# Diffusion step on one core: adaLN gates, scale and shift rows by broadcasting DMAs from DRAM instead of one-hot matmuls

## What is computed

```
sh_a, sc_a, g_a, sh_f, sc_f, g_f = _ada(c, w_ada[i], b_ada[i])
h = _modulate(x, sh_a, sc_a)                       # layernorm(x) * (1 + scale) + shift
...                                                # attention or Fourier mix, giving out
x = _post_norm(x, g_a * out, ln_gain[i, 0], ln_bias[i, 0])   # layernorm(ALPHA * x + g * out) * gain + bias
h = _modulate(x, sh_f, sc_f)
moe = _hier_moe(h, w_rg, w_re, w_g, w_u, w_d)
x = _post_norm(x, g_f * moe, ln_gain[i, 1], ln_bias[i, 1])
```

## Time and profile before

| | |
|---|---|
| median of 3 runs | 1095.87 us |
| profiled execution: its time, its span | 1099.61 us, 1097.9 us |
| PE busy | 862.1 us (79%) |
| PE weight loads busy | 463.3 us (42%) |
| VectorE, ScalarE, GpSimd busy | 349.5, 164.2, 140.1 us |
| DMA | 310.20 MB, mean 283 GB/s |
| mean granted TensorE clock | 0.912 |
| chain that ended last, by engine | PE 49%, DMA 33%, DVE 9%, SP's queue 4%, issue 4% |

### The profile page before, as it was taken

The page is one execution under the profiler, slowest core; times in us unless marked ns, Lnnn a source line. Parts: engine busy times, 40 slices in busy tenths (PEclk is TensorE's granted clock), DMA queues, the critical chain, the costliest instruction groups (busy, mean ns, idle before and its releaser), DMA issues.

```text
span 1097.9 us, 14316 instructions
## 1 busy us (share of the span) xinstructions
PE 862.1 (79%) x5177; PEld 463.3 (42%) x5178; DVE 349.5 (32%) x859; ACT 164.2 (15%) x339; POOL 140.1 (13%) x212
## 2 busy tenths in 40 slices
PE   3699999987996787988777864999679887877850
PEld 2465665655555332333323323675543333323320
DVE  2103656566365211111111117445521101111118
ACT  0112221122101111110111113210211111011110
POOL 1021111300000102111111110000011111111110
PEclk9799999999997698999998996999779989989985
DMA  8958163269945166799999929514939999999922
GB/s 324 367 149 278 48 231 139 101 216 386 367 185 198 42 244 281 301 420 419 420 421 400 419 78 388 213 39 162 395 136 419 420 419 420 418 421 412 394 106 104
DMA packets 91155, 310.20 MB, mean 283 GB/s; under 512 B 16398, under 2 KB 29022, under 8 KB 66536
## 3 DMA queue, kind: packets, MB, share of 16 engines
q1 hardware_dynamic: 69968, 275.12, 63.3%
q10 hardware_dynamic: 10392, 20.79, 5.2%
q0 software_dynamic: 10752, 13.70, 3.6%
HBM read 307.95 MB, written 26.74 MB: 305 GB/s over the span
## 4 chain that ended last, share of the span: by engine, by line
PE 49%; DMA 33%; DVE 9%; SPq 4%; issue 4%; ACT 1%; POOL 1%; POOLq 0%; DVEq 0%; ACTq 0%
DMA ring<-in_w_expert_up 23%; PE psum L772 14%; PE psum L668 10%; PE psum L636 8%; PE psum L794 3%; DMA ring<-in_w_ada 3%; PE psum L624 2%; PE psum L592 2%; DMA y_scratch<-arena,sidx 2%; DMA arena<-h_scratch,gidx 2%; SPq L388 1%; DMA ring<-in_w_qkv 1%; PE psum L759 1%; SPq L373 1%; PE psum L952 1%
## 5 line engine op out<-in xcount | busy, mean ns | idle before, releaser
L772 PE MATMUL psum<-ring,arena 128*64 128x512 f32 x1088 | 269.5, 652 | 56.2 <-DMA ring<-in_w_expert_up 52.2
L772 PEld LDWEIGHTS psum<-ring,arena 128*64 128x64 f32 x1088 | 96.0, 150 | 226.0 <-issue 223.7
L794 PE MATMUL psum<-ring,arena 128*64 128x512 f32 x544 | 125.8, 604 | 29.2 <-DVE arena L1496 27.9
L668 PE MATMUL psum<-ring,hT 128*128 128x384 f32 x384 | 130.7, 496 | 7.9 <-DMA ring<-in_w_qkv 7.9
L1492 DVE TENSOR_TENSOR arena<-arena,psum 128x256 f32<-128x256 f32 x34 | 14.3, 421 | 314.7 <-ACT arena L1054 314.7
L668 PEld LDWEIGHTS psum<-ring,hT 128*128 128x128 f32 x384 | 72.9, 194 | 55.8 <-DMA ring<-in_w_qkv 8.1
L636 PE MATMUL psum<-ring,hT 128*128 128x512 f32 x192 | 83.8, 593 | 0.0
L794 PEld LDWEIGHTS psum<-ring,arena 128*64 128x64 f32 x544 | 40.0, 138 | 91.6 <-issue 77.1
L592 PE MATMUL psum<-ring,silu 128*32 128x128 f32 x1536 | 52.5, 295 | 19.2 <-DMA ring<-in_w_ada 13.3
L1502 DVE COPY arena<-psum 128x512 f32<-128x512 f32 x34 | 23.5, 691 | 134.3 <-PE psum L794 134.3
L528 POOL DMA_INDIRECT y_scratch<-arena,sidx x34 | 34.3, 1010 | 190.0 <-DVE arena L1502 189.2
(11 more groups left out here) (158 smaller groups left out, 799.8 us busy)
## 6 DMA issues: line engine op xcount, KB each, us to landing
ring<-in_w_expert_gate SPq DMA_DIRECT2D x64, 1024.0 KB, 12.7
ring<-in_w_expert_up SPq DMA_DIRECT2D x64, 1024.0 KB, 18.6
ring<-in_w_expert_down SPq DMA_DIRECT2D x64, 1024.0 KB, 21.2
ring<-in_w_ada SPq DMA_DIRECT2D x24, 2048.0 KB, 16.8
ring<-in_w_qkv SPq DMA_DIRECT2D x12, 1024.0 KB, 16.8
h_scratch<-h ACTq DMA_DIRECT2D x6, 1024.0 KB, 4.8
arena<-y_scratch ACTq DMA_DIRECT2D x6, 1024.0 KB, 7.0
ring<-in_w_attn_out SPq DMA_DIRECT2D x2, 2048.0 KB, 20.6
```

The lines of the kernel that those rows point to most:

```text
L668: last = pe.matmul(bank[i % 2][:, 0:384], mem.hT[:, k, P * t:P * t + P], w[:, k, 384 * half:384 * half + 384], start=(k == 0), stop=(k == ...
L772: last = pe.matmul(bank[b][64 * e:64 * e + 64, :].rearrange("p (g n) -> p g n", g=2), mem.GT[b][:, c, 64 * e:64 * e + 64], w, start=(c == ...
L794: last = pe.matmul(bank[5 + half][64 * e:64 * e + 64, :], mem.actT[b][:, f, 64 * e:64 * e + 64], w[:, f, 512 * half:512 * half + 512], sta ...
```

## The change

All one-hot spreads go, with their table (`sel`), the gate evictions on ScalarE and their semaphores. GpSimd stores `m` to a DRAM scratch (`store_m`, only the two partitions of each group of 32 that carry the sets) and fills each row buffer by a DMA that reads 4 KB of that scratch for every partition. `lnscale` is a new buffer; `lnshift` takes the place of the third gather buffer. DVE waits for the DMAs and writes `h` in natural order; the transposes that feed router and experts (`turn` with `strided`, `gt`) read every eighth column instead. PE's order is simpler: `project` of tile 2 goes to banks 6 and 7, `turn` to banks 4 and 5. Of the constant table SP loads only the identity first (128 columns instead of 745); the rest (617 columns, before it was the 1024 of `sel`) follows the first qkv unit.

```
+        self.lnscale = sb("lnscale", [P, D])
...
+        self.lnshift = view(46, D)
...
+        m_dram = nc.dram_tensor("m_scratch", (2, 2, NMOD * D), F32).ap()
...
-            early = _C["sel"][0]
+            early = _C["ident"][1]
...
-                    sp.dma_start(mem.rows[:, early:], A["k_rows"][:, early:]).then_inc(selectors_in, 16)
+                    sp.dma_start(mem.rows[:, early:], A["k_rows"][:, early:]).then_inc(tables_in, 16)
...
+            stored = [0]
+
+            def store_m(l, first, last, ready):
+
+                pool.wait_ge(ada_done, ready)
+                for i in range(2):
+                    pool.dma_start(m_dram[l, i].rearrange("(u j n) -> j u n", j=4, n=P)[:, first:last, :],
+                                   mem.m[i:i + 97:32, l, first:last, :]).then_inc(m_out, 16)
+                stored[0] += 32
+                pool.wait_ge(m_out, stored[0])
+
+            def spread(dst, l, vec, i, done):
+
+                pool.dma_start(dst, m_dram[l, i, vec * D:vec * D + D].partition_broadcast(P)).then_inc(done, 16)
+
+            def norm_rows(l, i):
+                spread(mem.lnscale[:, :], l, 4, i, lnscale_in)
+                spread(mem.lnshift, l, 3, i, lnshift_in)
+
+            store_m(0, 4, ADA_UNITS, ADA_UNITS)
+            norm_rows(0, 0)
+            pool.wait_ge(pv_ps, STEPS)
+            for i in range(2):
+                spread(mem.gates[:, i, :], 0, 2, i, gates_in[i])
+            store_m(1, 4, 8, 20)
...
+                if l == 1:
+                    pool.wait_ge(norm_ready, 9)
+                    spread(mem.gates[:, 1, :], 1, 2, 1, gates_in[1])
+                    store_m(1, 8, ADA_UNITS, 2 * ADA_UNITS)
+                    norm_rows(1, 0)
                 for t in range(TILES):
                     for _ in range(2):
                         root([t])
+                    if t == 0:
+                        pool.wait_ge(norm_ready, 6 * l + 4)
+                        norm_rows(l, 1)
+                pool.wait_ge(proj_used, 6 * (l + 1))
+                for i in range(2):
+                    spread(mem.gates[:, i, :], l, 5, i, gates_in[i])
...
+                    if l == 0 and tiles == [0]:
+                        pool.wait_ge(norm_ready, 7)
+                        spread(mem.gates[:, 0, :], 1, 2, 0, gates_in[0])
...
-            def turn(t, banks):
+            def turn(t, banks, strided=False):
                 for c in range(KC):
-                    last = pe.transpose(bank[banks[c // 4]][:, P * (c % 4):P * (c % 4) + P],
-                                        mem.h[:, t, P * c:P * c + P], ident)
+                    src = mem.h[:, t, c::KC] if strided else mem.h[:, t, P * c:P * c + P]
+                    last = pe.transpose(bank[banks[c // 4]][:, P * (c % 4):P * (c % 4) + P], src, ident)
                     if c % 4 == 3:
                         last.then_inc(turn_ps, 1)
-
-            def spread(l, vec, i, banks):
-
-                for half in range(2):
-                    for j in range(4):
-                        last = pe.matmul(banks[half][:, P * j:P * j + P],
-                                         mem.const("sel")[:, P * (2 * j + i):P * (2 * j + i) + P],
-                                         mem.m[:, l, 2 * vec + half, :], start=True, stop=True)
-                return last
...
-                                        mem.G[b][:, P * c:P * c + P], ident)
+                                        mem.G[b][:, c::KC], ident)
...
             def mixer_to_experts(l):
                 if l == 0:
-                    pe.wait_ge(selectors_in, 16)
-                    spread(l, 2, 0, (bank[6], bank[7])).then_inc(gate_ps, 1)
-                    project(l, 0, (0, 1), (0,))
-                    spread(l, 2, 1, (bank[4], bank[5])).then_inc(gate_ps, 1)
-                    project(l, 0, (0, 1), (1,))
-                pe.wait_ge(gate_sb, 4 * l + 2)
-                spread(l, 4, 0, (bank[4], bank[5]))
-                spread(l, 3, 0, (bank[6], bank[7])).then_inc(rows_ps, 1)
+                    pe.wait_ge(tables_in, 16)
+                    project(l, 0, (0, 1))
                 project(l, 1, (2, 3))
-                pe.wait_ge(proj_used, 6 * l + 2)
-                project(l, 2, (0, 1), (0,))
+                project(l, 2, (6, 7), (0,))
                 pe.wait_ge(norm_ready, 6 * l + 4)
-                spread(l, 4, 1, (bank[4], bank[5]))
-                spread(l, 3, 1, (bank[6], bank[7])).then_inc(rows_ps, 1)
-                pe.wait_ge(proj_used, 6 * l + 4)
-                turn(0, (2, 3))
-                project(l, 2, (0, 1), (1,))
+                turn(0, (4, 5), strided=True)
+                project(l, 2, (6, 7), (1,))
                 pe.wait_ge(norm_ready, 6 * l + 5)
                 wait_turn(pe, TURN_ROUTE[l], 0)
-                turn(1, (2, 3))
+                turn(1, (4, 5), strided=True)
                 pe.wait_ge(router_in, 64)
-                pe.wait_ge(proj_used, 6 * (l + 1))
+                pe.wait_ge(proj_used, 6 * l + 2)
                 router(l, 0)
                 wait_turn(pe, TURN_ROUTE[l], 1)
                 router(l, 1)
                 pe.wait_ge(norm_ready, 6 * l + 6)
-                turn(2, (2, 3))
-
-                spread(l, 5, 0, (bank[6], bank[7])).then_inc(gate_ps, 1)
+                turn(2, (4, 5), strided=True)
                 wait_turn(pe, TURN_ROUTE[l], 2)
                 router(l, 2).then_inc(logits_ps, 1)
-                spread(l, 5, 1, (bank[4], bank[5])).then_inc(gate_ps, 1)
...
-                    dve.wait_ge(gate_sb, 4 * l + 1 + i)
+                    dve.wait_ge(gates_in[i], 16 * (2 * l + 1))
                     for half in range(2):
                         n, part = 6 * l + 2 * t + half + 1, slice(512 * half, 512 * half + 512)
                         dve.wait_ge(proj_ps, n)
-                        V.tensor_tensor(tmp[:, part], bank[(2 if t == 1 else 0) + half],
+                        V.tensor_tensor(tmp[:, part], bank[(0, 2, 6)[t] + half],
                                         mem.gates[:, i, part], ALU.mult).then_inc(proj_used, 1)
...
-                    dve.wait_ge(rows_ps, 2 * l + 1 + i)
-                    link(V.scalar_tensor_tensor(out=tmp, in0=x, scalar=mean, in1=mem.psum[:, 2048:2048 + D],
+                    dve.wait_ge(lnscale_in, 16 * (2 * l + 1 + i))
+                    link(V.scalar_tensor_tensor(out=tmp, in0=x, scalar=mean, in1=mem.lnscale[:, :],
                                                 op0=ALU.subtract, op1=ALU.mult))
-                    V.scalar_tensor_tensor(
-                        out=mem.h[:, t, :].rearrange("p (c k) -> p k c", c=KC),
-                        in0=tmp.rearrange("p (k c) -> p k c", c=KC), scalar=rstd,
-                        in1=mem.psum[:, 2048 + D:2048 + 2 * D].rearrange("p (k c) -> p k c", c=KC),
-                        op0=ALU.mult, op1=ALU.add).then_inc(norm_ready, 1)
+                    dve.wait_ge(lnshift_in, 16 * (2 * l + 1 + i))
+                    V.scalar_tensor_tensor(out=mem.h[:, t, :], in0=tmp, scalar=rstd,
+                                           in1=mem.lnshift,
+                                           op0=ALU.mult, op1=ALU.add).then_inc(norm_ready, 1)
...
+                    dve.wait_ge(gates_in[0 if t == 0 else 1], 16 * (2 * l + 2))
```

More of the change, by code:

```diff
@@ L93, in constants @@
     put("ones", np.ones((P, P)))
-    sel = np.zeros((P, 4, 2, P))
-    for j in range(4):
-        for i in range(2):
-            sel[32 * j + i, j, i, :] = 1.0
-    put("sel", sel)
     nf = HD // 4
@@ L278, in build @@
         lam_done, o_raw = sem("lam_done"), sem("o_raw")
-        gate_ps, gate_sb = sem("gate_ps"), sem("gate_sb")
+        gates_in = [sem(f"gates_in{i}") for i in range(2)]
+        m_out, lnscale_in, lnshift_in = sem("m_out"), sem("lnscale_in"), sem("lnshift_in")
         proj_ps, proj_used = sem("proj_ps"), sem("proj_used")
         gb_in, gb_used = sem("gb_in"), sem("gb_used")
-        rows_ps = sem("rows_ps")
         turn_ps, turn_lo, turn_hi = sem("turn_ps"), sem("turn_lo"), sem("turn_hi")
-        y_scaled, count_ps, selectors_in = sem("y_scaled"), sem("count_ps"), sem("selectors_in")
+        y_scaled, count_ps, tables_in = sem("y_scaled"), sem("count_ps"), sem("tables_in")
         logits_ps, route_in, route_out, pos_ps, msum_done = (
@@ L945, in _ @@
             pe.wait_ge(chan_dve, 4)
-            spread(1, 2, 1, (bank[4], bank[5])).then_inc(gate_ps, 1)
             pe.wait_ge(ada_done, 2 * ADA_UNITS)
@@ L976, in turn_evict @@
                 last.then_inc((turn_lo, turn_hi)[part], 1)
-            def gate_evict(n, i, banks):
-                act.wait_ge(gate_ps, n)
-                nc.scalar.copy(mem.gates[:, i, :], mem.psum[:, 512 * banks:512 * banks + D]).then_inc(gate_sb, 1)
             def load_norm(idx):
```

17 lines of the change are left out of this document (3 added, 14 removed).

## The result

The changed kernel took 1089.37 us (median of 4 runs, 1087.51 to 1090.47) beside 1096.19 us for the kernel before (4 runs): ratio 0.9936, 95% interval 0.9919 to 0.9953, 6.8 us faster. The profiled execution took 1089.52 us, its span is 1087.6 us, its mean granted clock 0.897 (0.912 before). The forecast was 6.9 us. The sum was right and several of its terms were not, so the stages are read one by one.

The account below looks back on a forecast made before the run. PE and weight DMA in turns were taken to bound the kernel. Start 0.9 + layer 0 4.0 + layer 1 9.8 - strided transposes 7.8 = 6.9 us, taken from 1095.87: 1089.0 us, range 1078 to 1099.

Parts of the forecast that it names:

- What bounds the kernel, and that a gain ahead of an expert stage arrives at the end: PE and weight DMA bound in turns; weights mostly pace expert stages, which shift whole, so time saved ahead reaches the end.
- DMA price in layer 0: Two pairs of row reads in the full weight stream cost 2.7 us each, pushing second output weights to 291.5 us.
- PE at half clock behind that gap: Sign of a wrong forecast: PE at 1.2 GHz after its new gap at 280 to 283 us, layer 0.
- The step's 1.4 us: Layer 0 projections: without spreads but with later output weights, the last one ends at 327.8 instead of 329.2 us.
- 1.9 of the 2.65 are gained: Layer 0, between last turn and router: removing the 2.65 us spread gains 1.9 us, eviction of the turned tile remaining.
- Strided transposes, 7.8 us: Router turns and expert gather groups: 128 transposes on the chain lose 0.061 us each through weight loads with 32-byte steps.
- steps are free: Rival, chance 0.18: strided transpose loads hide beneath the matmuls; gain 14.7 us, time 1081.2 us.
- Write of `h`: DVE tail of tile 2: the strided write of 1.96 us becomes 1.29 us, 0.7 us gained in each layer.
- Gather in layer 1, 2.5 us of loss: First gather of layer 1 meets expert loads and new gate rows; 2.5 us lost, bounds 0 and 4.6.
- Start, 0.9 us: Kernel start: first table load shrinks from 372 to 64 KB ahead of the weights, gaining 0.9 us.
- Refetches between tiles: Norm rows for tiles 1 and 2 are requested some 11 us before use: hidden, with 4 us to spare.
- The signs that were named: Trace signs for right (loads near 0.2 us, groups of 8 at 1.5 us, earlier logits) or wrong (groups unchanged, half clock).

Follow-up runs that it names:

- the DMAs alone: Changed kernel with the permuted write of `h` and contiguous transposes of before, so only DMAs in place of the spreads; 1090.53 us, ratio 0.993 to the kernel before.
- the gather's 5.87: Kernel with all layer 0 rows early and three groups of idle matmuls, its expert-layer gate rows now read after the first two gathers; 1072.83 us, ratio 0.9768.
- its own counterpart: Changed kernel with all layer 0 rows early and three groups of idle matmuls, gate rows still ahead of the gathers; 1073.29 us, ratio 0.9782.

## Why the prediction came out right, point by point

- **What bounds the kernel, and that a gain ahead of an expert stage arrives at the end:** right. Layer 1's stretch up to the norm gave 10.2 us where 10.5 were worked out, which is the larger part of the whole gain.
- **DMA price in layer 0 ("2.7 us for each pair", 5.4 together):** right in mechanism. Norm rows 2.8 us and gate rows 4.1 by the two runs with early rows, 6.9 together; against the kernel before the first projection came 6.4 us later. Wrong in the place: I let the second output weights bind, at 291.5 us. It was the first ones that PE waited for, from 274.7 to 281.52; into the second ones it ran at about 291.2 without a wait.
- **PE at half clock behind that gap:** named only among the signs of failure, with no price. It cost 2.6 us (the second half of tile 0 began 9.7 us after the first, not 7.1). The step's 1.4 us became 0.0: 6.4 and 2.6 lost, 8.9 of spreads saved.
- **"1.9 of the 2.65 are gained" between turn and router, and 1.8 in layer 1:** the step that failed most instructively. They became 0.0 and -0.3. I took the router behind the spread as unchanged; it went from 1.72 us to 3.61, since with the one-hot matmuls went what brought the clock back for it. The run with seven added matmuls in their place has it at 1.95 again (layer 0). Matmuls can pay for themselves by the clock of what follows.
- **Strided transposes, 7.8 us:** failed. 0.0075 us each in place of 0.061, about 1 us over 128. My own rival "steps are free" had the evidence for it in the earlier trace rows: 141 ns loads at 0.11 us spacing were already hidden. I weighed a pair of L780 above a stream of eight.
- **Write of `h`:** 0.7 us in layer 0, as worked out.
- **Gather in layer 1, 2.5 us of loss:** 2.0 measured, by the cause that was named, expert loads and gate rows that reach up to the gather; how the loss divides between the two is open. **Start, 0.9 us:** neither shown nor excluded. **Refetches between tiles:** hidden, as said; no engine of the chain after waits for them.
- **The signs that were named:** of those for right came loads near 0.2 us (193 ns), the first gather of layer 1 (5.4 us) and PE idle before the output weights came, the latter ahead of the first ones; the groups of eight did not reach 1.5 us, and the last router's logits came 3.5 and 13.4 us earlier by the profiles, not 5 and 17. Of those for wrong, two came: groups of eight nearly unchanged, and PE at half clock behind its new gap.
- What is still open: 1.1 us between the first gather transposes of layer 1 and the end. The run with the DMAs alone has it too (293.6 us there and after, 292.4 before), so it is not the steps'. In nine profiles with the DMAs and the gate rows ahead of the gathers this stretch takes 292.6 to 294.9 us, in four with the one-hot matmuls 291.3 to 292.7; I did not trace it further.

So the forecast of 6.9 us held by luck, because errors cancelled: some 7 us of loss by the steps that did not come, against gains of 1.4, 1.9 and 2.1 us that did not come either (weights and clock), up to 0.9 at the start, and 1.1 of loss that are open. A reader should trust the mechanisms that the runs confirm, not the total.

The best version of the study keeps the broadcasts, reads the rows of layer 0 ahead of the full stretch, and keeps TensorE busy across the router's gaps: 1073 us, 2.2 to 2.3% below the kernel before. About 7 us of the 24 are the change's, 7 the early rows', 10 the added matmuls'.

## What to carry to other kernels

Before removing matmuls, look at the granted clock of the matmuls behind them: here the router stood behind a turn at half clock, and without the one-hot matmuls between them it ran at half clock too. When reads are moved into DMA, look for the queue's last stretch with gaps ahead of where they are wanted, and issue them there: these rows cost some 7 us when read inside the full stretch. Price a longer weight load by the pace of its group, not by its own duration. And compare a variant's trace with that of the kernel it was made from: beside the changed kernel's 5.39 us the gather's 5.87 looked like no gain, beside its own counterpart's 8.06 it is 2.2 us shorter.

## What the runs showed of the hardware

- The fp32 weight loads of the gather transposes (128x128) take 141 ns contiguous and 193 ns with a step of 32 bytes; those of L780, with a step of 8 bytes, 202 ns; the contiguous ones of the projections 190 ns. A stream of eight transposes keeps its pace with the step of 32 bytes (1.04 to 1.10 us).
- TensorE ran at 1.2 GHz behind 6.8 and 6.6 us of idleness, in the kernel before also behind 3.8 us (the positions). In the second profile of that kernel the positions of layer 1 took 1.52 us behind 3.85 us of idleness, so full clock. Behind 2.72 us it began at 2.4 GHz, behind 2.79 and 3.46 us in two other runs partly at 1.2. Matmuls of no use, placed in the gaps, took 6.5 us from a kernel of 1090.
- The first qkv matmul began between 41.8 and 45.2 us in nine profiles of programs with one and the same start.
- A gather of the same size took 3.4 us in the chain at a DMA share of 0.19, 5.4 us at 0.70 and 8.1 us at 0.76.
